# Shift products with the shift columns stationary, and their rows of sums turned by matmuls with ones

## The chip, the core and the metric

The kernel runs on one core of a Trainium2 chip. A core has five engines with queues of their own: TensorE (PE; its weight loads are shown apart as PEld), VectorE (DVE), ScalarE (ACT), GpSimd (POOL) and SyncE (SP), the last mostly for starting DMAs. They wait for one another by semaphores. The metric is the time on the device of one execution, in microseconds; smaller is better.

## What is computed

Two layers of a decoder trunk on 512 tokens of width 1024, in float32. Every layer has three blocks (an FFN, a mixing block with attention and convolution, an FFN), and every block begins with a norm that is scaled and shifted by columns drawn from a vector c:

```python
def rms_norm(x, g):
    xf = x.astype(jnp.float32)
    y = xf * lax.rsqrt(jnp.mean(xf * xf, axis=-1, keepdims=True) + EPS)
    return (y * g.astype(jnp.float32)).astype(x.dtype)

def modulate(h, shift, scale):
    return h * (1 + scale[:, None, :]) + shift[:, None, :]
...
        h = modulate(rms_norm(x, ffn1_norm[l]), sh1, sc1)
        x = x + 0.5 * g1[:, None, :] * swiglu(h, ffn1_w_in[l], ffn1_w_out[l])

        h = modulate(rms_norm(x, mix_norm[l]), sh2, sc2)
        proj = h @ w_mix_in[l]
...
        h = modulate(rms_norm(x, ffn2_norm[l]), sh3, sc3)
        x = x + 0.5 * g3[:, None, :] * swiglu(h, ffn2_w_in[l], ffn2_w_out[l])
```

All matrices are sums of three products of rounded parts, high by high, high by low and low by high, which keeps float32's precision on TensorE's faster float32r path.

## The kernel before

Activations lie turned: 128 channels on the partitions, 512 tokens in the free dimension, `KT` = 8 tiles for the width of 1024. A weight slab is 1024 x 128, held as `[128, 8, 128]`. SP loads it into `raw[slot]`, ScalarE rounds it to `whi[slot]` (`w_hi_part`, L435), VectorE takes the rest into `wlo[slot]` (`w_lo_part`, L790), and TensorE makes 3 x 8 products of 512 columns from it (`slab`, L1501 to L1503). Slabs come in pairs, slot 0 and slot 1; `w_hi`, `w_lo`, `w_used` count them.

Where a block begins (an *entry*), TensorE doesn't wait for the norm. It takes the first pair of slabs on the plain x, scaled by the norm's gain but neither divided by the root nor shifted (`plain_hi`, `plain_lo`). VectorE later multiplies what comes out by the row `RSTD` (`read_bank`, L873), and the shift's part is added as a column for each slab, `wshift` = slab^T times shift. The second pair of an entry takes the real normed and shifted tiles, one "unit" of 128 channels after another: VectorE `unit_gain` (L825), ScalarE `unit_hi` (L454), VectorE `unit_lo` (L834). There are five such entries: mix, second FFN, then in layer 1 first FFN, mix, second FFN.

On TensorE an entry is two calls of `two_slabs` (L1506). Slot 1 runs four steps behind slot 0. In the first call each step holds, besides its three products of 512 columns, two shift products (L1526, L1527): the weight slice (high, then low part) is stationary, and the two columns `SHP[:, shift, n, :]` (high and low part of the shift) move. They sum up in `S[slot][:, 0:2]`; VectorE adds the two columns at the end of its `norm_units` (L910). At k == 3 the mean of the squares is made (`norm_mean`, L1636). Before it can be used there follow ScalarE's root (L442) and VectorE's reciprocal (L814).

VectorE's order in an entry is written out by hand: unit gains and lows 0 to 2, read bank 0, rest of the next weights of slot 0, low of unit 3, read bank 1, gain of unit 4, rest of the weights of slot 1, gain of unit 5, low of unit 4, and so on. ScalarE's order is unit highs with two weight roundings in between (`ENTRY_SPLITS`).

The *first entry* is made otherwise, since the shift comes late (its columns are computed from `ada_w`). Two pairs are done on the plain x (`plain_slabs`), and `third_pair` (L1567) takes the third pair on the units. The shift products of the first two pairs (four slabs, 32 products of two matmuls) are put among its 16 turns, two products to a turn, into the banks `S[0]`, `S[1]`, `O`, `AUX`; in the first four steps two products with a tile of ones (`keep_busy`, L1646) are added at the end of each. After it the loop of FFN tiles begins with `slab(3, 0)`, which writes bank `G[0]` and so waits for `acc_read[0]`. That is counted up by VectorE's L935 in `first_gates`, and before L935 VectorE's queue holds L921 (which waits for ScalarE's tanh, L565), L924, the weights' rest, L928, L930 and L933, in that order.

Of the kernel before, what the change touches and what calls it, by code (L numbers as in the profile page):

```python
# [124 lines left out]
def build(nc, a, onehot, out):  # L125
# [28 lines left out]
    whi = [at(f"w_hi{s}", [P, 8, P], F32R) for s in range(2)]  # L154
    wlo = [at(f"w_lo{s}", [P, 8, P], F32R) for s in range(2)]
# [31 lines left out]
    wshift = at("w_shift", [P, 2], F32)  # L187
    busy = at("busy", [P, TOK], F32R)
# [45 lines left out]
    whi_next = [at(f"w_hi_next{s}", [P, 8, P], F32R, r0 + 64 * KB + s * 4 * KB) for s in range(2)]  # L234
    wlo_next = [at(f"w_lo_next{s}", [P, 8, P], F32R, r0 + 72 * KB + s * 4 * KB) for s in range(2)]
# [183 lines left out]
    def _(act):  # L419
# [36 lines left out]
        def norm_units(l, k, pair):  # L456
# [6 lines left out]
            for j in range(KT):  # L463
# [6 lines left out]
                if j in ENTRY_SPLITS and not first:  # L470
                    w_hi_part(pair + 1, ENTRY_SPLITS[j])

# [84 lines left out]
        for l in range(DEPTH):  # L557
            for w in range(2):
                n_in, n_out = f"ffn{w + 1}_in", f"ffn{w + 1}_out"
                norm_units(l, 2 * w, l * PAIRS + PAIR0[n_in])  # L560
                if l + w == 0:
                    w_hi_part(3, 0, used=1)
                    act.wait_ge(sem("first_gate"), 1)
# [222 lines left out]
    def _(dve):  # L786
# [74 lines left out]
        def norm_units(l, k, pair, rows):  # L861
# [44 lines left out]
            low(7)  # L906
            for t in range(2):
                if first:
                    dve.wait_ge(w_used[t], 1)
                dve.tensor_scalar(wshift[:, t:t + 1], S[t][:, 0:1], S[t][:, 1:2], rows[t], ALU.add, ALU.mult)\  # L910
                    .then_inc(sem("shift_read"), 1)

        def first_gates():
# [15 lines left out]
            dve.wait_ge(w_used[0], 2)  # L929
            dve.tensor_scalar(wshift_next[:, 0:1], O[:, 0:1], O[:, 1:2], 1.0, ALU.add, ALU.mult).then_inc(sem("shift_read_next"), 1)  # L930
# [14 lines left out]
            dve.tensor_scalar(wshift_next[:, 1:2], AUX[:, 0:1], AUX[:, 1:2], 1.0, ALU.add, ALU.mult)\  # L945
                .then_inc(sem("shift_read_next"), 1)
            dve.wait_ge(sem("shift_read_next"), 2)
# [542 lines left out]
    def _(pe):  # L1490
# [14 lines left out]

        def two_slabs(pair, use, ready, shift=None, at={}, banks=G, weights=(whi, wlo)):  # L1506

            lag = 4
            for k in range(KT + lag):
                if k in at:  # L1510
                    at[k]()
                for slot, n in ((1, k - lag), (0, k)):
# [12 lines left out]
                    if shift is not None:  # L1525
                        pe.matmul(S[slot][:, 0:2], wh, SHP[:, shift, n, :], start=n == 0, stop=False)  # L1526
                        pe.matmul(S[slot][:, 0:2], wl, SHP[:, shift, n, :], start=False, stop=n == KT - 1)  # L1527
# [31 lines left out]
        def shift_product(slot, n, out, weights):  # L1559
# [3 lines left out]
            if n == KT - 1:  # L1563
                mm.then_inc(w_used[slot], 1)
# [354 lines left out]
```

## Time and profile before

| | |
|---|---|
| median of 3 runs | 2539.62 us (2538.05 to 2539.93) |
| profiled execution, its own time | 2538.0 us |
| its span | 2536.3 us |
| TensorE busy | 2511.7 us, 99% |
| VectorE busy | 1687.4 us, 67% |
| ScalarE busy | 968.0 us, 38% |
| mean granted TensorE clock | 0.998 |

A matmul's busy time is modelled and overlaps the next one's, so 99% doesn't mean that nothing could be saved; the distance between the starts of two neighbours is what a product costs. A row of the timeline gives start, busy time, engine, line, operation, out<-in, shape and in brackets the idle time before it with what ended it. A row of the chain gives start, length and what the end of the execution hung on then.

### The profile page before, as it was taken

What the parts mean: (1) busy time and instruction counts of PE and PEld (TensorE: products, weight loads), DVE (VectorE), ACT (ScalarE), POOL (GpSimd) and SP (SyncE); (2) the same over time, 40 slices, a digit from 0 to 9 for tenths busy, and PEclk for the clock granted to TensorE, in tenths of its full rate; (3) what the DMA queues carried; (4) which work ended last, traced back from release to release, by engine and by line L of the source; (5) the groups of instructions that cost most, each with busy time, mean ns of one, the idle gap of its engine ahead of it and who ended that gap; (6) DMA issues with size and microseconds to landing.
All of it is one profiled execution on the core that took longest, in us unless ns stands there. A gap on an engine that the chain in (4) does not pass through costs nothing.

```text
span 2536.3 us, 34970 instructions
## 1 busy us (share of the span) xinstructions
PE 2511.7 (99%) x11607; PEld 2049.3 (81%) x11607; DVE 1687.4 (67%) x2531; ACT 968.0 (38%) x1630; POOL 108.2 (4%) x187
## 2 busy tenths in 40 slices
PE   8999999999999999999999999999999999999998
PEld 6888887878788878888878888877877888788887
DVE  8655678899987575643365557788999865634432
ACT  4322324454545342232232332255455443432223
POOL 3000110000000000000000001100000000000000
PEclk9999999999999999999999999999999999999999
DMA  9555574232223435533335556722222333333332
GB/s 279 156 166 158 187 241 119 83 87 82 86 84 91 133 91 159 156 102 97 92 100 158 156 166 191 232 80 83 86 84 79 88 100 94 89 99 96 92 99 86
DMA packets 467654, 310.99 MB, mean 123 GB/s; under 512 B 10891, under 2 KB 445181, under 8 KB 467576
## 3 DMA queue, kind: packets, MB, share of 16 engines
q1 hardware_dynamic: 444544, 234.91, 31.7%
q0 software_dynamic: 20352, 70.13, 8.6%
q10 hardware_dynamic: 2696, 5.13, 0.7%
q8 instruction: 38, 0.62, 0.1%
q14 instruction: 24, 0.20, 0.0%
HBM read 305.41 MB, written 5.05 MB: 122 GB/s over the span
## 4 chain that ended last, share of the span: by engine, by line
PE 92%; DVE 4%; ACT 2%; issue 1%; DMA 1%; POOL 0%; ACTq 0%; DVEq 0%; POOLq 0%
PE bank L1501 28%; PE bank L1503 28%; PE bank L1502 28%; PE bank L1803 2%; PE bank L1781 1%; DVE rstd L814 1%; DVE scaled L825 1%; PE bank L1773 1%; DVE h_lo L834 1%; DVE w_lo L790 1%; PE bank L1523 1%; PE bank L1528 0%; PE bank L1524 0%; PE bank L1811 0%; PE bank L1789 0%
## 5 line engine op out<-in xcount | busy, mean ns | idle before, releaser
L790 DVE TENSOR_TENSOR w_lo<-w_raw,w_hi 128x1024 fp32r<-128x1024 f32 (+1 forms) x428 | 514.9, 1203 | 539.8 <-ACT w_hi L435 539.0
L1501 PE MATMUL bank<-h_hi,w_hi 128*128 128x512 f32 x2096 | 833.3, 398 | 0.3 <-DVE scaled L1150 0.2
L1503 PE MATMUL bank<-h_hi,w_lo 128*128 128x512 f32 x2096 | 817.6, 390 | 0.0
L1502 PE MATMUL bank<-h_lo,w_hi 128*128 128x512 f32 x2096 | 816.3, 389 | 0.0
L435 ACT ACTIVATE w_hi<-w_raw 128x1024 fp32r<-128x1024 f32 (+1 forms) x428 | 445.3, 1040 | 847.3 <-PE bank L1503 796.3
L1501 PEld LDWEIGHTS bank<-h_hi,w_hi 128*128 128x128 f32 x2096 | 393.6, 188 | 85.8 <-issue 4.2
L1503 PEld LDWEIGHTS bank<-h_hi,w_lo 128*128 128x128 f32 x2096 | 393.4, 188 | 84.5
L1502 PEld LDWEIGHTS bank<-h_lo,w_hi 128*128 128x128 f32 x2096 | 394.1, 188 | 77.3 <-issue 0.5
L1266 DVE SCALAR_TENSOR_TENSOR conv_part<-glu,conv_taps,conv_part 128x512 f32<-128x512 f32 x464 | 319.7, 743 | 0.0
L1501 PE MATMUL bank<-s_hi,w_hi 128*128 128x512 f32 x704 | 275.5, 391 | 0.0
L1503 PE MATMUL bank<-s_hi,w_lo 128*128 128x512 f32 x704 | 274.0, 389 | 0.0
L1502 PE MATMUL bank<-s_lo,w_hi 128*128 128x512 f32 x704 | 273.9, 389 | 0.0
L1503 PEld LDWEIGHTS bank<-s_hi,w_lo 128*128 128x128 f32 x704 | 132.2, 188 | 27.7
L1502 PEld LDWEIGHTS bank<-s_lo,w_hi 128*128 128x128 f32 x704 | 132.2, 188 | 26.9
L1501 PEld LDWEIGHTS bank<-s_hi,w_hi 128*128 128x128 f32 x704 | 132.2, 188 | 26.9
L989 DVE SCALAR_TENSOR_TENSOR ada_acc<-ada_raw,c_act,ada_acc 128x1024 f32<-128x1024 f32 x112 | 143.3, 1280 | 0.9
L389 POOL DMA_DIRECT2D ada_raw<-in_ada_w x128 | 69.0, 539 | 1153.0 <-DVE ada_acc L986 544.5
L594 ACT ACTIVATE s_hi<-full 128x512 f32 (+1 forms) x82 | 51.9, 632 | 162.4 <-DVE full L1158 162.4
L1160 DVE TENSOR_TENSOR s_lo<-full,s_hi 128x512 f32 (+1 forms) x82 | 56.8, 692 | 73.9 <-ACT s_hi L594 73.9
L494 ACT ACTIVATE squares<-x_res 128x512 f32 (+1 forms) x48 | 30.3, 632 | 194.6 <-DVE x_res L972 194.6
L677 ACT ACTIVATE probs<-probs,neg_row_max 128x512 f32<-128x512 f32 (+3 forms) x128 | 71.0, 556 | 74.2 <-DVE neg_row_max L1303 73.9
L972 DVE SCALAR_TENSOR_TENSOR x_res<-bank,gates,x_res 128x512 f32 (+1 forms) x48 | 36.0, 751 | 68.0 <-PE bank L1503 67.8
(271 smaller groups left out, 2682.7 us busy)
## 6 DMA issues: line engine op xcount, KB each, us to landing
w_raw<-in_ffn_w_in SPq DMA_DIRECT2D x176, 512.0 KB, 3.9
ada_raw<-in_ada_w POOLq DMA_DIRECT2D x128, 512.0 KB, 4.8
w_raw<-in_w_mix_in SPq DMA_DIRECT2D x112, 512.0 KB, 3.7
w_raw<-in_ffn_w_out SPq DMA_DIRECT2D x64, 512.0 KB, 3.9
w_raw<-in_ffn_w_out SPq DMA_DIRECT2D x32, 384.0 KB, 3.5
ada_first<-in_ada_w SPq DMA_DIRECT2D x16, 512.0 KB, 9.0
w_raw<-in_w_attn_branch SPq DMA_DIRECT2D x16, 512.0 KB, 3.8
w_raw<-in_w_conv_branch SPq DMA_DIRECT2D x16, 512.0 KB, 3.8
```

The lines of the kernel that those rows point to most:

```text
L389: pool.dma_start(ada_raw[k % 4][:, :], w_ada[:, ds(layer * KT + k, 1), ds(m * D, D)].rearrange("p o f -> p (o f)"))\
L435: act.activation(whi[slot][:, 0:n, :], raw[slot][:, 0:n, :], ACT.Copy).then_inc(w_hi[slot], 1)
L594: act.activation(tile(SHI2, i), F[0][:, :], ACT.Copy).then_inc(sem("s_hi"), 1)
L677: act.activation(PR[par][m][:, 0:n], PR[par][m][:, 0:n], ACT.Exp, bias=nmx[:, par, m:m + 1], scale=-1.0, accum_out=rsum[:, par, m:m + 1]). ...
L790: dve.tensor_tensor(wlo[slot][:, 0:n, :], raw[slot][:, 0:n, :], whi[slot][:, 0:n, :].bitcast(F32), ALU.subtract).then_inc(w_lo[slot], 1)
L989: ins = dve.scalar_tensor_tensor(out=ACC[:, :], in0=ada_raw[k % 4][:, :], scalar=CA[:, k:k + 1], in1=ACC[:, :], op0=ALU.mult, op1=ALU.add)
L1160: dve.tensor_tensor(tile(SLO2, i), F[0][:, :], tile(SHI2, i).bitcast(F32), ALU.subtract)\
L1266: ins = dve.scalar_tensor_tensor(out=CAB[t % 2][:, :], in0=Z[:, t:t + TOK], scalar=wt, in1=CAB[t % 2][:, :], op0=ALU.mult, op1=ALU.add)
L1501: pe.matmul(acc, wh, hi[:, k0 + k, :], start=first and k == 0, stop=False)
L1502: pe.matmul(acc, wh, lo[:, k0 + k, :], start=False, stop=False)
L1503: mm = pe.matmul(acc, wl, hi[:, k0 + k, :], start=False, stop=last and k == n - 1)
L1803: mm = pe.matmul(S[m][:, 0:n], q[m * HD:(m + 1) * HD, i * P:(i + 1) * P], k[m * HD:(m + 1) * HD, 0:n], start=term == 0, stop=term == 2)
```

## The change

The roles of the two operands are exchanged. The two shift columns of a tile are stationary now, and 256 weight columns, 128 of each slot, move. The result is two rows of 256 sums, for the high and the low part of the shift, in `S[0][0:2, 0:256]`. ScalarE copies them to SBUF, and two matmuls with two of the ones of `busy` turn each slot's 2 x 128 block into a column of 128 and add its two rows. For this the weight tiles of the two slots lie in one tensor, `w_both`.

In the entries the eight tiles' products (two matmuls each) stand at k = 5, 6 and 7 of the first call of `two_slabs`; ScalarE's copy stands after unit 4; the two turning matmuls (`entry_sums`) stand at k == 6 of the second call, into `S[1][:, 0:2]`, where VectorE reads them after the last unit. In the first entry turns 0 to 3 of `third_pair` take two tiles each of the first pair's weights and turns 4 to 11 one tile each of the second's, with one `keep_busy` instead of two. There the first copy is at unit 4 and `entry_sums` at k == 6. The second copy stands in ScalarE's queue between the rounding of pair 3, slot 0, and the tanh, and waits for turn 11; its two matmuls stand at k == 10.

```diff
@@ sbuf
-    whi = [at(f"w_hi{s}", [P, 8, P], F32R) for s in range(2)]
-    wlo = [at(f"w_lo{s}", [P, 8, P], F32R) for s in range(2)]
+    w_both = [at(f"w_{part}", [P, 2, 8, P], F32R) for part in ("hi", "lo")]
+    whi, wlo = [[both[:, s, :, :] for s in range(2)] for both in w_both]
@@ scalar, norm_units
                 if j in ENTRY_SPLITS and not first:
                     w_hi_part(pair + 1, ENTRY_SPLITS[j])
+                if j == KT // 2:
+                    if first:
+                        act.wait_ge(w_used[1], 1)
+                    else:
+                        act.wait_ge(sem("shift_rows"), l * 3 + k)
+                    act.activation(shift_rows[0:2, :], S[0][0:2, 0:2 * P], ACT.Copy).then_inc(sem("shift_rows_copied"), 1)
@@ scalar, first FFN
                 if l + w == 0:
                     w_hi_part(3, 0, used=1)
+                    act.wait_ge(w_used[1], 2)
+                    act.activation(shift_rows_next[0:2, :], O[0:2, 0:2 * P], ACT.Copy).then_inc(sem("next_rows_copied"), 1)
                     act.wait_ge(sem("first_gate"), 1)
@@ vector, norm_units
+            dve.wait_ge(sem("shift_sums"), l * 3 + k + 1)
             for t in range(2):
-                if first:
-                    dve.wait_ge(w_used[t], 1)
-                dve.tensor_scalar(wshift[:, t:t + 1], S[t][:, 0:1], S[t][:, 1:2], rows[t], ALU.add, ALU.mult)\
-                    .then_inc(sem("shift_read"), 1)
+                dve.tensor_scalar(wshift[:, t:t + 1], S[1][:, t:t + 1], rows[t], None, ALU.mult).then_inc(sem("shift_read"), 1)
@@ vector, first_gates
-            dve.wait_ge(w_used[0], 2)
-            dve.tensor_scalar(wshift_next[:, 0:1], O[:, 0:1], O[:, 1:2], 1.0, ALU.add, ALU.mult).then_inc(sem("shift_read_next"), 1)
+            dve.wait_ge(sem("next_sums"), 1)
+            dve.tensor_copy(wshift_next[:, :], AUX[:, 0:2]).then_inc(sem("shift_read_next"), 1)
...
-            dve.tensor_scalar(wshift_next[:, 1:2], AUX[:, 0:1], AUX[:, 1:2], 1.0, ALU.add, ALU.mult)\
-                .then_inc(sem("shift_read_next"), 1)
-            dve.wait_ge(sem("shift_read_next"), 2)
@@ tensor
+        def shift_product(n, shift, out, weights):
+
+            pe.matmul(out[0:2, 0:2 * P], SHP[:, shift, n, :], weights[0][:, :, n, :], start=n == 0, stop=False)
+            return pe.matmul(out[0:2, 0:2 * P], SHP[:, shift, n, :], weights[1][:, :, n, :], start=False, stop=n == KT - 1)
+
+        def shift_sums(out, rows):
+
+            for t in range(2):
+                mm = pe.matmul(out[:, t:t + 1], rows[0:2, t * P:(t + 1) * P], busy[0:2, 0:1].bitcast(F32), start=True, stop=True)
+            return mm
+
+        def entry_sums(n):
+
+            pe.wait_ge(sem("shift_rows_copied"), n + 1)
+            shift_sums(S[1], shift_rows).then_inc(sem("shift_sums"), 1)
@@ tensor, two_slabs
+                if shift is not None and lag < k < KT:
+                    for n in range(3 * (k - lag - 1), min(3 * (k - lag), KT)):
+                        mm = shift_product(n, shift, S[0], w_both)
+                    if k == KT - 1:
+                        mm.then_inc(sem("shift_rows"), 1)
...
-                    if shift is not None:
-                        pe.matmul(S[slot][:, 0:2], wh, SHP[:, shift, n, :], start=n == 0, stop=False)
-                        pe.matmul(S[slot][:, 0:2], wl, SHP[:, shift, n, :], start=False, stop=n == KT - 1)
@@ tensor, third_pair
+                if k == 6:
+                    entry_sums(0)
+                if k == 10:
+                    pe.wait_ge(sem("next_rows_copied"), 1)
+                    shift_sums(AUX, shift_rows_next).then_inc(sem("next_sums"), 1)
...
-                    for part in range(2):
-                        i = 2 * turn + part
-                        out, pair_weights = products[i // KT]
-                        shift_product(i // KT % 2, i % KT, out, pair_weights)
-                        if part == 0:
-                            pe.matmul(acc, wh, HLO[:, n, :], start=False, stop=False)
+                    if turn < lag:
+                        for m in (2 * turn, 2 * turn + 1):
+                            last = shift_product(m, 0, S[0], w_both)
+                        if turn == lag - 1:
+                            last.then_inc(w_used[0], 1)
+                    elif turn < lag + KT:
+                        last = shift_product(turn - lag, 0, O, next_both)
+                        if turn == lag + KT - 1:
+                            last.then_inc(w_used[0], 1)
+                    rest = pe.matmul(acc, wh, HLO[:, n, :], start=False, stop=False)
+                    if turn in (lag - 1, lag + KT - 1):
+                        rest.then_inc(w_used[1], 1)
...
                     if k < lag:
-                        keep_busy(2, S[1])
+                        keep_busy(1, S[1])
@@ tensor, entry
-                      banks=G if name == "mix" else TP)
+                      at={6: lambda: entry_sums(n)}, banks=G if name == "mix" else TP)
```

## Rows read from the trace of the kernel before

**Rows 1.** The page's part 4: shares of the chain by engine.

```profile
PE 92%; DVE 4%; ACT 2%; issue 1%; DMA 1%; POOL 0%; ACTq 0%; DVEq 0%; POOLq 0%
```

**Rows 2.** Chain in order of time (start, length, what), l0 mix entry.

```profile
403.69 0.76 DVE x_res L972
...
423.18 0.67 DVE h_lo L834
...
423.90 0.50 PE bank L1523
...
431.85 0.29 issue
```

**Rows 3.** The same chain in the l1 ffn2 entry.

```profile
2155.21 0.76 DVE x_res L972
...
2175.30 0.50 PE bank L1523
```

**Rows 4.** Timeline (start, busy, what) of TensorE, first pair of an entry.

```profile
404.25 0.40 PE L1523 MATMUL bank<-h_hi,w_hi 128*128 128x512 f32 x1
...
405.17 0.39 PE L1523 MATMUL bank<-h_hi,w_hi 128*128 128x512 f32 x1
...
418.61 0.48 PE L1528 MATMUL bank<-h_hi,w_lo 128*128 128x512 f32 x1
419.56 0.47 PE L1523 MATMUL bank<-h_hi,w_hi 128*128 128x512 f32 x1 [0.48 <-issue]
```

**Rows 5.** Timelines of TensorE, VectorE and ScalarE, first entry.

```profile
54.20 0.47 PE L1581 MATMUL bank<-h_hi,w_hi_third 128*128 128x512 f32 x1 [0.95 <-DVE h_lo L834]
...
65.25 0.39 PE L1581 MATMUL bank<-h_hi,w_hi_third 128*128 128x512 f32 x1
...
66.39 0.39 PE L1581 MATMUL bank<-h_hi,w_hi_third 128*128 128x512 f32 x1
...
74.32 0.39 PE L1501 MATMUL bank<-h_hi,w_hi 128*128 128x512 f32 x1
...
60.84 0.75 DVE L834 SCALAR_TENSOR_TENSOR h_lo<-scaled,modulation,h_hi 128x512 fp32r<-128x512 f32 x1
...
68.58 0.68 DVE L921 SCALAR_TENSOR_TENSOR scaled<-scaled,full 128x512 f32<-128x512 f32 x1
...
72.36 0.68 DVE L935 SCALAR_TENSOR_TENSOR scaled<-scaled,bank 128x512 f32<-128x512 f32 x1
...
66.25 0.63 ACT L565 ACTIVATE scaled<-full 128x512 f32<-128x512 f32 x1
```

**Rows 6.** Timeline of TensorE around score products of 256 and 128 columns.

```profile
478.59 0.28 PE L1803 MATMUL bank<-k_lo,q_hi 64*128 64x256 f32 x2
478.70 0.28 PE L1803 MATMUL bank<-k_hi,q_lo 64*128 64x256 f32 x2
...
484.78 0.39 PE L1503 MATMUL bank<-h_hi,w_lo 128*128 128x512 f32 x1
...
485.92 0.39 PE L1502 MATMUL bank<-h_lo,w_hi 128*128 128x512 f32 x1
```

**Rows 7.** ScalarE: a group by line and shape (busy, mean ns), and its timeline.

```profile
L643 ACT ACTIVATE weights_t<-bank 128x256 f32<-128x256 f32 x16 | 6.2, 385 | 6.5 <-PE bank L1773 6.5
...
423.27 0.72 ACT L454 ACTIVATE h_hi<-scaled,modulation 128x512 fp32r<-128x512 f32 x1 [1.07 <-DVE scaled L825]
```

**Rows 8.** One line's instructions: ns min/median/max, first and last start, L1889.

```profile
L1889 PE MATMUL bank<-inv_d,squares x8: 250/250/271, 2526.6 to 2527.4; 128*128 128x1 f32 x8
```

**Rows 9.** Timelines of VectorE and TensorE, end of the l0 mix entry.

```profile
431.35 0.68 DVE L1342 TENSOR_TENSOR k_lo<-squares,k_hi 128x512 fp32r<-128x512 f32 x1
...
432.13 0.50 PE L1803 MATMUL bank<-k_hi,q_hi 64*128 64x512 f32 x2 [0.29 <-issue]
```

**Rows 10.** Stretches: busy us of each engine, granted clock, DMA share, GB/s.

```profile
13.00:15.50 2.50, 0.07 (x1) 0.00 (x0) 2.25 (x2) 0.00 (x0) 0.00 (x0) 1.00 1.04 386
16.00:20.00 4.00, 4.00 (x16) 3.14 (x14) 3.83 (x4) 0.51 (x1) 0.00 (x0) 0.57 1.03 410
```

More of the change, by code:

```diff
@@ L187, in build @@
     wshift = at("w_shift", [P, 2], F32)
+    shift_rows = at("shift_rows", [P, 2 * P], F32)
     busy = at("busy", [P, TOK], F32R)
@@ L232, in build @@
     CAB = [at(f"conv_part{i}", [P, TOK], F32, z0 + 2176 + 2 * KB * i) for i in range(2)]
-    whi_next = [at(f"w_hi_next{s}", [P, 8, P], F32R, r0 + 64 * KB + s * 4 * KB) for s in range(2)]
-    wlo_next = [at(f"w_lo_next{s}", [P, 8, P], F32R, r0 + 72 * KB + s * 4 * KB) for s in range(2)]
+    next_both = [at(f"w_{part}_next", [P, 2, 8, P], F32R, r0 + (64 + i * 8) * KB) for i, part in enumerate(("hi", "lo"))]
+    whi_next, wlo_next = [[both[:, s, :, :] for s in range(2)] for both in next_both]
+    shift_rows_next = at("shift_rows_next", [P, 2 * P], F32, r0 + 62 * KB)
     whi_third = [at(f"w_hi_third{s}", [P, 8, P], F32R, r0 + 16 * KB + s * 4 * KB) for s in range(2)]
@@ L1557, in plain_slabs, with third_pair @@
                         mm.then_inc(sem("plain_read"), 1)
-        def shift_product(slot, n, out, weights):
-            pe.matmul(out[:, 0:2], weights[0][slot][:, n, :], SHP[:, 0, n, :], start=n == 0, stop=False)
-            mm = pe.matmul(out[:, 0:2], weights[1][slot][:, n, :], SHP[:, 0, n, :], start=False, stop=n == KT - 1)
-            if n == KT - 1:
-                mm.then_inc(w_used[slot], 1)
-        def third_pair(banks, weights, products):
+        def third_pair(banks, weights):
             lag = 4
@@ L1581, in third_pair @@
                     pe.matmul(acc, wh, HHI[:, n, :], start=n == 0, stop=False)
-                    for part in range(2):
-                        i = 2 * turn + part
-                        out, pair_weights = products[i // KT]
-                        shift_product(i // KT % 2, i % KT, out, pair_weights)
-                        if part == 0:
-                            pe.matmul(acc, wh, HLO[:, n, :], start=False, stop=False)
+                    if turn < lag:
[10 more added lines that the diff above has]
+                        rest.then_inc(w_used[1], 1)
                     mm = pe.matmul(acc, wl, HHI[:, n, :], start=False, stop=n == KT - 1)
-                    turn += 1
                     if n == KT - 1:
@@ L1592, in third_pair @@
                     if k < lag:
-                        keep_busy(2, S[1])
+                        keep_busy(1, S[1])
+                    turn += 1
         def first_entry():
@@ L1604, in first_entry @@
             pe.wait_ge(sem("aux_read"), 1)
-            third_pair(G, thirds, ((S[0], (whi, wlo)), (S[1], (whi, wlo)), (O, nexts), (AUX, nexts)))
+            third_pair(G, thirds)
         def entry(l, k, name):
```

## The prediction

> **What bounds the kernel now.** I read the page's chain first [rows 1]: TensorE carries 92% of it, so taking matmuls away looks like taking time away. That share is an average. I therefore took the chain in order of time in the two kinds of place that the edit touches: the five entries (l0 mix at 403 us, l0 ffn2 at 912, l1 ffn1 at 1279, l1 mix at 1647, l1 ffn2 at 2155) and the first entry at 54 to 74 us.
>
> In an entry [rows 2] the chain leaves TensorE when the last x tile is updated at 403.69, goes through root, reciprocal and the unit scalings on ScalarE and VectorE, and comes back to TensorE only at 423.90, when the fifth unit's low part (begun 423.18) is there. From 423.90 on, the second pair of slabs is the chain to its end at 431.85. The other four entries have the same links; the last goes from 2155.21 to 2175.30 [rows 3], 20.1 us as against 20.2. The shift products that go lie in the *first* pair, inside the stretch in which VectorE sets the end. TensorE finishes that pair about 0.5 us early: its last product starts at 418.61, and the next pair's first at 419.56 after 0.48 us idle [rows 4]. In the first entry it is the reverse: TensorE is the chain without a gap from 54.20 to 74.32 [rows 5].
>
> **Change, part by part. The entries, first pair.** A step (slot, k) with its two shift products takes 405.17 - 404.25 = 0.92 us [rows 4]; a plain product is 0.23 (from the chain [rows 2]: 431.85 less 423.90, less 0.50 for the first, over 32), so the two 2-column products cost 0.23 together, 0.115 each, and 32 of them 3.7 us. In their place stand 16 products of 256 columns. The nearest rows are the score products with 256 moving columns: neighbours start at 478.59 and 478.70, 0.11 apart [rows 6]. They have a 64-row stationary block and run as two side by side, so that it is the step of a pair; I take 0.115, 1.8 us in all. TensorE is done some 1.9 us sooner, but the second pair's fifth step still waits for 423.9. **Worth nothing**: next late after TensorE is VectorE's fixed order, which waits nowhere for TensorE in this stretch. ScalarE's copy of the two rows (2 x 256; the nearest row, 128 x 256 out of a bank, takes 0.385 [rows 7]) goes between unit 4 and unit 5, where ScalarE sat idle 1.07 us for VectorE [rows 7]: hidden; without that cover it would cost 0.4 on the chain.
>
> **The entries, second pair.** New at k == 6, in the middle of the chain: two matmuls that turn the rows. They are plain f32; such a one runs as two instructions (the means at the end: 8 for 4 matmuls, last start 0.8 after first, 0.115 each [rows 8]), so four of them are 0.46. Their stationary block has 2 of 128 rows. The nearest rows for a block of few rows amid full ones are the last scores: from the product at 484.78 to the next but one at 485.92 is 1.14 us, where two plain steps are 0.46 and the three side-by-side pairs of 128 columns 0.34; 0.34 is left for going over and back [rows 6]. So the sums cost 0.46 to 0.80; being narrow I take 0.80. A waiting bubble of some 0.08 at unit 6 and another after the pair, where TensorE waited for VectorE, swallow up to 0.15.
> The Trainium skill, "TensorEngine Tiling (Array Packing)", Key Properties, says that a change of the array's tiling mode drains the engine; that speaks against this change, and the 0.34 above agrees. Against it, "TensorE: Matmul & The Clock Gate", Back-to-back issue gap, gives a floor of about 25 ns for small matmuls by themselves, by which the four would be an estimated 0.1 us; the row of the means shows 115 ns with a load for each, so the sum goes by the row. By the page's floor the entries would add nothing and the whole would come to about 2539, inside the range.
> - Three ffn entries: about +0.6 each, **+1.8**. VectorE's readers of the sums come after the last unit, over 0.5 us behind TensorE's k == 6, so the wait for them holds up nothing.
> - Two mix entries: after the pair the score products already waited for k_lo (431.35 + 0.68 = 432.03) and began at 432.13 [rows 9], 0.28 after the chain says that the pair was through [rows 2]. Of 0.65 some 0.25 is left, twice: **+0.4**. Bound for all five: 0 to +4.0.
>
> **The first entry.** Before, a step is 66.39 - 65.25 = 1.14 us [rows 5]: three products and four of 0.115. After, turns 0 to 3 have four of the new ones and one busy product instead of two: 0.69 + 0.46 + 0.23 = 1.38. With turn 4 that is 54.20 + 4 x 1.38 + 0.92 = 60.6, so turn 5 still starts when unit 4 is low (60.84 + 0.75, so about 61.7 [rows 5]). Seven turns at 0.92 and the sums, 0.8, bring turn 11 to about 68.9; four bare steps and the second sums end the pair near 72.4 instead of 74.32. Taken alone, 1.9 us gained. But the change puts a wait in ScalarE's queue: after w_hi of pair 3, slot 0, it waits for w_used[1] of turn 11 and then copies the rows (68.9 + 0.385, so 69.25). **Queued behind it** is the first tanh (66.25 before), and behind that VectorE's L921 (68.58) and, by a fixed row of instructions, L935 (72.36 to 73.04), which alone frees bank G[0] for TensorE's next slab [rows 5]. Tanh at 69.25 and 0.63 long puts L921 at 69.95, 1.35 late, and L935's end at 74.4. TensorE starts the next slab at 74.5 instead of 74.32: **+0.2**, not -1.9. The gain is traded for a wait. Bounds: with sums at 0.46 it is -0.15; with dearer products, below.
>
> Sum: 1.8 + 0.4 + 0.2 = +2.4 us, on the profiled execution's 2538.0 (span 2536.3 and 1.7 around it) 2540.4. That execution was 1.6 under the median of the three runs, 2539.6; against the median **2542.0 us**. About 5 us, 0.2%, is what a measurement of this kernel can tell from no change.
>
> **Rivals.**
> 1. *TensorE is the bound everywhere.* Then every freed slot counts: per entry -3.7 + 1.8 + 0.8 = -1.1, five times -5.4; in the first entry 64 x 0.115 and 4 busy products less 32 x 0.115 and twice 0.8, so -3.0. Total -8.4: 2531. For it the 92% [rows 1]; against it the entries' chain and its slack, which show who is waited for [rows 2 to 5]. Chance 0.06.
> 2. *The clock.* (The slower side.) From 13.08 to 15.50 TensorE stood still, and the granted clock, full until then, was 0.57 in the mean from 16 to 20 us although TensorE was busy throughout [rows 10]: the lower level, 1.2 GHz, for most of it, and 0.43 x 4 = 1.7 us of work lost. Later, up to its last work, TensorE's longest pause is the 0.95 us at 54.20 [rows 5]. The change makes longer ones: 1.9 us before the second pair in each entry, 2.0 us before slab 3 in the first. If the clock falls, an entry loses up to 1.7 less the slack of its first steps (423.90 - 419.56 for 15 products at 0.23, so 0.9), so about 1.0, and the first entry 1.7: 2542.0 + 5 + 1.7 = 2548.7; in the first alone, 2543.7. It decides only if the clock answers these pauses as it did that one, which was longer (2.4 us) and stood among sparser work. Chance of the full form 0.15.
> 3. *The 2-column stationary block costs a change of mode too.* 0.34 per group: hidden in the entries (three groups, 1.0 us, of 1.9), but in the first entry twelve groups: turns 0 to 3 at 1.72 end near 61.1, eight turns at 1.26 and the sums near 71.9, 3.0 later than above: 2545.0. The same comes out if a new product takes 0.2. The 2-column moving form can't show it. Chance 0.11.
> 4. *The sums run at the low end and the bubbles take most:* 2540. Part of the forecast's range.
>
> **How the numbers follow.** Forecast, with rival 4 in it: 0.66; rival 1: 0.06; rival 2: 0.15; rival 3: 0.11; 0.02 for none of these. Range: from the forecast without its terms, 2538.5, to just short of the full clock case, 2548.0; rival 1 and half of rival 2 are left out. Slower by over 5 us (above 2544.7): most of rival 2, half of rival 3, 0.17; faster by as much (under 2534.5): rival 1, 0.05; within: 0.78.
>
> **What would show it.** The chain of after must again leave TensorE from the x update to unit 4's low part, 20.2 us in each entry; TensorE must show a pause near 1.9 us before the second pair. The 256-column products must start 0.11 to 0.12 apart, the four sum instructions must widen k == 6 by 0.5 to 0.8. In the first entry the tanh of L565 must start near 69.2 behind the copy, and TensorE stand idle from about 72.4 until the bank is free near 74.4. A granted clock under 1.00 after 60 us would mean rival 2; an L935 end near 77, rival 3. A second pair beginning its fifth step sooner than 20.2 us after the x update would overturn the reading of the entries.

## The result and the profile after

| | before | after |
|---|---|---|
| median | 2539.09 us (2537.74 to 2540.60, 17 runs) | 2543.48 us (2541.71 to 2545.91, 17 runs) |
| profiled execution, its own time | 2538.0 us | 2541.71 us |
| its span | 2536.3 us | 2539.7 us |
| mean granted clock | 0.998 | 0.998 |

The changed kernel takes 1.0016 of the time before (95% interval 1.0008 to 1.0023), so +4.4 us between the medians, against +2.4 forecast over a base of 2539.6. It is slower, by a little less than the 5 us that the prediction had called measurable; the interval leaves out 1, so that threshold was set too high.

The page of the changed kernel, its busy times and the shares of its chain by engine:

```profile
PE 2504.5 (99%) x11519; PEld 2032.6 (80%) x11519; DVE 1686.7 (66%) x2530; ACT 969.7 (38%) x1637; POOL 108.4 (4%) x187
...
PE 91%; DVE 5%; ACT 2%; issue 1%; DMA 1%; POOL 0%; ACTq 0%; DVEq 0%; POOLq 0%
```

TensorE's busy time went down by 7.2 us and the span went up by 3.4. Where, is seen as for before [rows 1 to 5]. The chain of the changed kernel in the l0 mix entry (start, length, what):

```profile
404.34 0.76 DVE x_res L977
...
423.82 0.67 DVE h_lo L844
424.54 0.49 PE bank L1549
...
426.95 0.53 PE bank L1519 x4
```

From the x update to the second pair's fifth step are again 20.20 us (424.54 - 404.34), as before [rows 2]: nothing of TensorE's saving came through. The last row is new. It is the sums, on the chain.

TensorE's timeline of the same entry (start, busy time, what, idle time before and its releaser):

```profile
406.75 1.10 PE L1663 MATMUL bank<-running_sum,inv_d 128*128 128x512 f32 x2 [0.56 <-issue]
...
409.78 0.28 PE L1513 MATMUL bank<-w_hi,shift_parts 128*2 128x256 f32 x1
409.89 0.28 PE L1514 MATMUL bank<-w_lo,shift_parts 128*2 128x256 f32 x1
...
418.30 0.39 PE L1551 MATMUL bank<-h_hi,w_lo 128*128 128x512 f32 x1
420.21 0.47 PE L1549 MATMUL bank<-h_hi,w_hi 128*128 128x512 f32 x1 [1.52 <-DVE w_lo L800]
...
426.56 0.40 PE L1551 MATMUL bank<-h_hi,w_lo 128*128 128x512 f32 x1
426.88 0.60 PE L1519 MATMUL bank<-busy,shift_rows 2*128 2x1 f32 x4
...
427.75 0.40 PE L1550 MATMUL bank<-h_lo,w_hi 128*128 128x512 f32 x1
...
433.07 0.50 PE L1830 MATMUL bank<-k_hi,q_hi 64*128 64x512 f32 x2
```

Six of the new products fill 409.78 to 410.47 (the next plain product), 0.115 each. The freed time stands as idle time in two places: 0.56 at 406.75, where the mean now has to be waited for and before stood no wait (counted from start to start, 405.80 to 406.75, it is 0.95 where a plain step is 0.23, so 0.72), and 1.52 ahead of the second pair instead of 0.48 [rows 4]. From the product before the sums to the second one behind them are 1.19 us (427.75 - 426.56) where two plain steps are 0.46: the sums cost 0.73.

The first entry in the changed kernel, rows of TensorE, VectorE and ScalarE, as in [rows 5]:

```profile
54.86 0.47 PE L1602 MATMUL bank<-h_hi,w_hi_third 128*128 128x512 f32 x1 [1.41 <-DVE h_lo L844]
...
72.90 0.39 PE L1615 MATMUL bank<-h_hi,w_lo_third 128*128 128x512 f32 x1
75.26 0.47 PE L1506 MATMUL bank<-h_hi,w_hi 128*128 128x512 f32 x1 [1.97 <-DVE scaled L943]
...
70.61 0.69 DVE L929 SCALAR_TENSOR_TENSOR scaled<-scaled,full 128x512 f32<-128x512 f32 x1 [1.06 <-ACT scaled L575]
...
74.33 0.68 DVE L943 SCALAR_TENSOR_TENSOR scaled<-scaled,bank 128x512 f32<-128x512 f32 x1
...
69.60 0.37 ACT L572 ACTIVATE shift_rows_next<-bank 2x256 f32<-2x256 f32 x1 [2.51 <-PE bank L1612]
69.88 0.62 ACT L575 ACTIVATE scaled<-full 128x512 f32<-128x512 f32 x1
```

TensorE starts 0.66 later than in [rows 5] (54.86, not 54.20). Its start follows ScalarE's rounding of an earlier tile of weights, which waits for that tile to land, by 19.9 us in every profile. Before, then changed:

```profile
34.28 1.06 ACT L423 ACTIVATE w_hi_next<-w_raw 128x1024 fp32r<-128x1024 f32 x1 [0.62 <-DMA w_raw<-in_ffn_w_in]
34.94 1.06 ACT L425 ACTIVATE w_hi_next<-w_raw 128x1024 fp32r<-128x1024 f32 x1 [1.09 <-DMA w_raw<-in_ffn_w_in]
```

The edit doesn't touch that transfer. Yet of the five profiles of the kernel before and of its variants below, four start the entry at 54.13 to 54.73 and one at 56.09, and the nine of the change and its variants at 54.60 to 55.27. Whether the change moves the landing stays open. Counted from the entry's start, the next slab begins after 20.40 us instead of 20.12.

With that the profile's +3.4 us closes: 0.66 for the start, 0.28 for the first entry, -0.29 from there to the l0 mix x update (329.08 instead of 329.37), and 2.75 from that update to the end (2135.36 instead of 2132.61).

### The profile page after: what moved, and what is told of

It reads as the page before. It is cut to its first block, busy times and chain, and to the rows that moved or that the text cites. A ratio compares the mean times of both kernels' runs of the same rounds, so it can differ in the third digit from the quotient of the medians.

```text
span 2539.7 us, 34799 instructions
## 1 busy us (share of the span) xinstructions
PE 2504.5 (99%) x11519; PEld 2032.6 (80%) x11519; DVE 1686.7 (66%) x2530; ACT 969.7 (38%) x1637; POOL 108.4 (4%) x187
## 4 chain that ended last, share of the span: by engine, by line
PE 91%; DVE 5%; ACT 2%; issue 1%; DMA 1%; POOL 0%; ACTq 0%; DVEq 0%; POOLq 0%
PE bank L1506 28%; PE bank L1508 28%; PE bank L1507 28%; PE bank L1830 2%; PE bank L1808 1%; DVE rstd L824 1%; DVE scaled L835 1%; DVE h_lo L844 1%; DVE w_lo L800 1%; PE bank L1800 1%; PE bank L1549 1%; PE bank L1551 0%; PE bank L1550 0%; PE bank L1838 0%; PE bank L1816 0%
## 5 line engine op out<-in xcount | busy, mean ns | idle before, releaser
L800 DVE TENSOR_TENSOR w_lo<-w_raw,w_hi 128x1024 fp32r<-128x1024 f32 (+1 forms) x428 | 514.9, 1203 | 542.4 <-ACT w_hi L437 541.6
L994 DVE SCALAR_TENSOR_TENSOR ada_acc<-ada_raw,c_act,ada_acc 128x1024 f32<-128x1024 f32 x112 | 143.3, 1280 | 0.9
```

Source lines behind the costliest of these rows:

```text
L800: dve.tensor_tensor(wlo[slot][:, 0:n, :], raw[slot][:, 0:n, :], whi[slot][:, 0:n, :].bitcast(F32), ALU.subtract).then_inc(w_lo[slot], 1)
L994: ins = dve.scalar_tensor_tensor(out=ACC[:, :], in0=ada_raw[k % 4][:, :], scalar=CA[:, k:k + 1], in1=ACC[:, :], op0=ALU.mult, op1=ALU.add)
```

## The experiments

Three sets were timed against the kernel before, each set on one chip, and one pair for profiles alone. Of the 101 executions of the kernel before, five lay at 2557 us; a profile of one stands under what was unexpected, and the medians are untouched by them.

**Is TensorE the bound in the entries after all (rival 1)?** In the kernel before, only tile 0's shift products are left in the five entries, so the shift is not the full one:

```diff
-                    if shift is not None:
+                    if shift is not None and n == 0:
```

> The kernel before, in whose five entries only tile 0 of the eight keeps its shift products (4 of 32 matmuls with 2 moving columns for each entry stay); the other tiles' part of the shift column is left out of the result. The theory (the entry's first pair lies under VectorE's chain): no time gained beyond 0.3 us, from the x update to the second pair's fifth step again 20.1 to 20.2 us in every entry, only TensorE's pause before the second pair grows from 0.5 to some 3.7 us. The rival (TensorE is the bound everywhere): 28 x 0.115 x 5 = 16 us faster than before. The clock's rival: the pause of 3.7 us brings the granted clock down behind it in some entries, at most 1.0 to 1.7 us each, so up to 8 us slower than before.

Measured: 2543.06 us (2541.85 to 2562.95, 11 runs), ratio 1.0015 (1.0005 to 1.0024). With 28 of an entry's 32 small matmuls gone, the kernel is *slower*. The pause ahead of the second pair grows to 3.3 us, and behind it the granted clock is half. TensorE's timeline in the l0 mix entry, and a stretch behind the pause (busy us of each engine, granted clock, DMA share, GB/s); this execution ran 18 us late, for the reason given at the end:

```profile
435.23 0.39 PE L1528 MATMUL bank<-h_hi,w_lo 128*128 128x512 f32 x1
438.87 0.77 PE L1523 MATMUL bank<-h_hi,w_hi 128*128 128x512 f32 x1 [3.26 <-DVE w_lo L790]
...
439.00:442.00 3.00, 3.00 (x8) 2.32 (x8) 3.00 (x5) 0.72 (x1) 0.00 (x0) 0.50 0.52 143
```

The same fall stood in all five entries, twice as long in l1 mix as in the others. The fifth step comes 20.96 us after the x update (443.96 - 423.00), not 20.2 as expected, since the first products behind the pause stand 0.43 apart and not 0.23. That leaves two readings: the freed slots are worth nothing and the clock costs the time by which the kernel is slower (3.8 us), or they are worth something and the clock takes more. So the pause was filled, with 24 products of ones that nothing reads:

```diff
+                      at={0: lambda: busy_part(12, TP[1])},
```

> The kernel before with the shift products of tile 0 alone in the five entries (fourteen pairs of them left out of each entry, so the shift is not the full one), and in the pause that opens ahead of each second pair 24 products of ones with 256 columns, 2.8 of the 3.3 us, read by nothing. The same without the filling gave 2543.06, 3.8 over the kernel before, with half-speed stretches of 3.41 us after the pauses of all five entries. Theory (the entries are bounded by VectorE's row, and the 3.8 us were the clock's): with the pauses filled there is no half-speed stretch after 60 us, and the time is that of the kernel before within 1 us, so 2538.5 to 2540.5. Rival (TensorE's freed slots are worth time, and the clock's fall merely hid it): clearly under the kernel before, down to 16 us.

Measured: 2538.72 us (2538.04 to 2539.82, 10 runs), ratio 0.9997 (0.9988 to 1.0007), and the granted clock is full from 17 us to the last work. TensorE in the l0 mix entry:

```profile
419.73 0.28 PE L1652 MATMUL bank<-busy 128*128 128x256 f32 x1
420.41 0.47 PE L1523 MATMUL bank<-h_hi,w_hi 128*128 128x512 f32 x1 [0.41 <-issue]
...
424.75 0.50 PE L1523 MATMUL bank<-h_hi,w_hi 128*128 128x512 f32 x1 [0.34 <-DVE h_lo L834]
```

The fifth step comes 20.21 us after the x update (424.75 - 404.54), products or no products, and the whole entry takes what it took before (table below). So the entries hang on VectorE, and rival 1 is out.

The 3.8 us were not the clock's alone. By the table the five entries of the unfilled run are 2.6 us longer than before. The same profile has two waits for late weights behind them, 1.20 us at 1037.72 and 1.41 at 1406.46, of the kind that is taken up under "What varies"; the filled run has none over 0.2 there. How much of the medians' difference is either's isn't separated.

**Are the entries' sums the loss?** They are moved into TensorE's pause, from k == 6 to k == 0 of the second pair, and ScalarE's copy from unit 4 to unit 1:

```diff
-                if j == KT // 2:
+                if j == (KT // 2 if first else 1):
...
-                      at={6: lambda: entry_sums(n)}, banks=G if name == "mix" else TP)
+                      at={0: lambda: entry_sums(n)}, banks=G if name == "mix" else TP)
```

> The changed kernel with the turning matmuls of the five entries moved from k == 6 of the second pair, in TensorE's chain, to its start, in TensorE's pause; ScalarE's copy goes from behind unit 4 to behind unit 1. The theory (the sums' place costs 0.66 us in an ffn entry and 0.3 in a mix entry): 3 x 0.66 + 2 x 0.3 = 2.6 us less than the changed kernel, some 1.5 us over before. The rival (the products and the first entry cost it): no difference from the changed kernel, 4 us over before.

Measured: 2539.92 us (2539.18 to 2542.45, 11 runs), ratio 1.0004 (0.9995 to 1.0013). The timeline shows them where TensorE waits for VectorE anyway:

```profile
420.23 0.39 PE L1551 MATMUL bank<-h_hi,w_lo 128*128 128x512 f32 x1
420.55 0.60 PE L1519 MATMUL bank<-busy,shift_rows 2*128 2x1 f32 x4
422.15 0.47 PE L1549 MATMUL bank<-h_hi,w_hi 128*128 128x512 f32 x1 [1.01 <-DVE w_lo L800]
```

The whole loss in the entries is the place of four small instructions: by the table below the five entries take no longer than before. The gain, 3.6 us against the changed kernel's 2543.5, is 0.7 more than the 2.8 by which the table has the entries shorter than in the change. The runs of one kernel spread over 3 to 5 us, so a difference of 0.7 between sets isn't read.

The counter-proof, the entries' sums made twice:

```diff
+            if n:
+                shift_sums(S[1], shift_rows)
```

> The changed kernel with the turning matmuls of the five entries done twice in a row at k == 6. If the price is in the matmuls (0.115 each with its load), the four extra instructions add 0.46 in each entry, 2.3 us over the changed kernel, all of it on the chain; if it is all in each one's narrow block, 0.80 each, 4.0 us; if the sums are nearly free (25 ns each), 0.5 us.

Measured: 2546.10 us (2543.98 to 2547.02, 10 runs), 2.6 over the 2543.5 of the change; by the table 2.2 in the entries, against 2.3 expected. In its l0 mix entry:

```profile
428.89 0.39 PE L1553 MATMUL bank<-h_hi,w_lo 128*128 128x512 f32 x1
429.21 1.05 PE L1519 MATMUL bank<-busy,shift_rows 2*128 2x1 f32 x8
...
430.52 0.40 PE L1552 MATMUL bank<-h_lo,w_hi 128*128 128x512 f32 x1
```

1.63 us (430.52 - 428.89) instead of 1.19: four more cost 0.44, so 0.11 each, and of the 0.73 some 0.27 is paid once for a group.

**Is that 0.27 the narrow block?** The entries' two rows are put in a tile of 128 rows whose other 126 POOL sets to zero once, so that the block is 128 by 128:

```diff
+            m = P if rows is shift_rows else 2
...
-                mm = pe.matmul(out[:, t:t + 1], rows[0:2, t * P:(t + 1) * P], busy[0:2, 0:1].bitcast(F32), start=True, stop=True)
+                mm = pe.matmul(out[:, t:t + 1], rows[0:m, t * P:(t + 1) * P], busy[0:m, 0:1].bitcast(F32), start=True, stop=True)
```

> The change, with the two rows of sums in a tile of 128 rows whose other 126 are zero, so that the four sum instructions of each entry have a stationary block of 128 by 128 in place of 2 by 128. In the change, the step with the sums is 1.19 us long where two plain products are 0.46: 0.73, of it 0.46 for four instructions at 0.115 and 0.27 for something else. Theory A (the 0.27 is the way into a block of 2 rows and back): the step shrinks to about 0.92, five times 0.27 less where nothing hides it, so 0.8 to 1.3 us under the change. Theory B (it comes with any small f32 product amid the large ones): the same step and the same time.

Measured: 2541.18 us (2540.58 to 2543.83, 12 runs), beside 2543.79 (2540.57 to 2545.23, 12 runs) for the change itself in the same set:

> The change as it is, run beside the next three so that they are compared on one chip. Theory (what the trace of it showed: 0.65 for the sums in each of three ffn entries, 0.3 in each of two mix entries, 0.4 in the first entry, 0.3 outside the span, and a part that varies from run to run): 2543.5, within 0.7.

```profile
427.00 0.39 PE L1554 MATMUL bank<-h_hi,w_lo 128*128 128x512 f32 x1
427.23 0.50 PE L1522 MATMUL bank<-busy,shift_rows 128*128 128x1 f32 x4
...
427.92 0.40 PE L1553 MATMUL bank<-h_lo,w_hi 128*128 128x512 f32 x1
```

0.92 us (427.92 - 427.00), 0.27 less: going over to a block of 2 rows and back is what it cost (both operands have 128 rows now, so the run doesn't tell the stationary one from the moving one), and four small f32 instructions by themselves are 0.46. The Trainium skill, "TensorEngine Tiling (Array Packing)", Key Properties, has the array drain at a change of mode, which agrees with these 0.27 if a block of 2 rows counts as another mode; the trace doesn't name modes.

The medians differ by 2.6 us, twice what was expected (0.8 to 1.3); drawing runs anew from both, by 0.4 to 3.5. They bear out the direction only. The size is read from the entries. From the x update to TensorE's first product behind the second pair (scores in the mix entries, the next slab in the others), us, in one profile each:

| | l0 mix | l0 ffn2 | l1 ffn1 | l1 mix | l1 ffn2 | sum over before |
|---|---|---|---|---|---|---|
| before | 28.44 | 27.89 | 27.92 | 28.46 | 27.90 | |
| changed | 28.73 | 28.55 | 28.58 | 28.77 | 28.56 | +2.58 |
| sums early | 28.32 | 27.89 | 27.93 | 28.32 | 27.90 | -0.25 |
| sums twice | 29.21 | 28.99 | 28.99 | 29.21 | 29.00 | +4.79 |
| full rows | 28.49 | 28.29 | 28.29 | 28.49 | 28.29 | +1.24 |
| tile 0 alone | 28.53 | 28.35 | 28.36 | 29.61 | 28.35 | +2.59 |
| tile 0 alone, pause filled | 28.45 | 27.89 | 27.92 | 28.45 | 27.91 | +0.01 |

The two further profiles of the kernel before and the two of the change repeat their rows within 0.04 us.

**Does ScalarE's copy hold up the first entry?** It is put behind the tanh and the next weights' rounding:

```diff
                     w_hi_part(3, 0, used=1)
-                    act.wait_ge(w_used[1], 2)
-                    act.activation(shift_rows_next[0:2, :], O[0:2, 0:2 * P], ACT.Copy).then_inc(sem("next_rows_copied"), 1)
...
                     w_hi_part(3, 1, used=1)
+                    act.wait_ge(w_used[1], 2)
+                    act.activation(shift_rows_next[0:2, :], O[0:2, 0:2 * P], ACT.Copy).then_inc(sem("next_rows_copied"), 1)
```

> The changed kernel with ScalarE's second copy of rows (and its wait for turn 11) moved behind the first tanh and the rounding of pair 3, slot 1. The theory: VectorE's first product with the tanh no longer waits for it and starts about 1.1 us sooner, so does the reading of bank 0, and TensorE's next slab starts near 74.2 instead of 75.3: 1.1 us less than the changed kernel, its pause 0.9 instead of 2.0 us. The rival (the bank was held by the row of VectorE's instructions, not by the copy): no difference.

Measured: 2541.89 us (2540.81 to 2545.78, 11 runs), 1.6 under the change. Rows of ScalarE, VectorE and TensorE (this execution begins the entry at 55.27):

```profile
67.03 1.06 ACT L437 ACTIVATE w_hi<-w_raw 128x1024 fp32r<-128x1024 f32 x1 [1.31 <-DMA w_raw<-in_ffn_w_in]
68.00 0.61 ACT L573 ACTIVATE scaled<-full 128x512 f32<-128x512 f32 x1
...
68.13 1.23 DVE L800 TENSOR_TENSOR w_lo<-w_raw,w_hi 128x1024 fp32r<-128x1024 f32 x1 [0.96 <-ACT w_hi L437]
...
70.47 0.68 DVE L929 SCALAR_TENSOR_TENSOR scaled<-scaled,full 128x512 f32<-128x512 f32 x1
...
75.11 0.47 PE L1506 MATMUL bank<-h_hi,w_hi 128*128 128x512 f32 x1 [1.41 <-DVE scaled L943]
```

The tanh starts 12.7 us after the entry's start instead of 15.0, but VectorE is then late itself: L929 follows L926 with no gap, 15.2 instead of 15.75, and the slab comes after 19.84 us instead of 20.40. So 0.56 came of the move, half of the 1.1 expected. VectorE's row was late because its L800 waited 0.96 for a tile of weights that landed later here: that rounding starts 11.8 us after the entry's start, in the change 11.2. In the change's own profile VectorE stood idle for 1.06 ahead of L929, which is what the move could give with the weights landing as there. The other 1.0 between the medians has a candidate in the next point: the pause is 1.41 us here, not 1.97.

**The clock in the first entry.** In the changed kernel TensorE stands still for 1.97 us ahead of the slab. Seven products of ones go in there:

```diff
             third_pair(G, thirds)
+            keep_busy(7, S[0])
```

> The change, with seven more products of ones at the end of the first entry's pair (their result is read by nothing), so that TensorE works through 1.6 of the 2.0 us for which it waits for the bank of the next slab. Theory A (the clock falls after this pause in a good part of the executions, as it did in the profiles of the runs with the sums early and with the sums twice, and not in those of the change itself and of the copy later): no half-speed stretch after 60 us, and a median 0.5 to 1.5 us under that of the change. Theory B (the clock plays no part in the median; what varies is something else): the same as the change within 0.4 us, or 0.1 more.

Measured: 2542.65 us (2541.54 to 2543.57, 12 runs). That is 1.1 under the change in the same set; drawing runs anew from both, the difference of the medians lies between -2.0 and +0.6, so the medians alone don't settle whether the clock plays a part in them, and the one profile of this run, at full clock, doesn't either, since the change's first two are so too. A third profile of the changed kernel was taken, with one of the kernel before:

> A third profile of the changed kernel, for the same question. Theory A: the loop of l0 ffn2 takes anywhere from 367.2 to 369.0. Theory B: 367.9 to 369.0, with the wait for late weights.

> A third profile of the kernel before. In the loop of l0 ffn2 (from the x update near 913 us to the one near 1280 us) the two profiles of it took 366.5 and 366.9 us and showed no wait for late weights over 0.2 us; the changed kernel and its variants, their own 0.65 us for the sums taken off, took 366.7 to 368.3 and showed a wait of 1.0 to 1.5 us in seven of eight. Theory A (chance of the execution): this profile falls anywhere in 366.5 to 368.3. Theory B (it goes with the changed kernel): 366.5 to 367.0 again.

The former took 2545.3 us. Two stretches of it behind the pause (its slab starts at 75.52 after 1.97 us):

```profile
77.00:79.00 2.00, 2.00 (x6) 1.54 (x5) 1.96 (x8) 1.04 (x2) 0.00 (x0) 0.50 0.01 2
81.00:84.00 3.00, 3.00 (x15) 2.47 (x14) 0.00 (x1) 1.10 (x2) 1.54 (x3) 1.00 0.76 239
```

At 1.2 GHz for a few microseconds: from the slab to the l0 mix x update it needs 330.75 us (406.27 - 75.52), where the first profile needs 329.08 (404.34 - 75.26) and the second 329.21, at full clock throughout. So 1.6 us, and the two profiles of variants in which it fell there need 330.97 and 330.96. With a pause of 1.97 to 2.42 us it fell in three of six profiles (this one, the sums early, the sums twice) and not in the other three (the two of the change, the full rows); with 1.41 us (copy later), 0.39 (filled) or none it did not, in one profile each.

**What varies in the loop of l0 ffn2.** From its x update near 913 us to the next near 1280, the profiles of the kernel before take 366.5, 366.9 and 366.8 us, those of the changed one 367.4, 368.3 and 368.9. The sums explain 0.65. The rest is one wait of TensorE, at 1016 to 1023, for weights that landed late. The second profile of the kernel before answers first:

> The kernel before as it is, for a second profile of it. In the profiles of every kernel of the two sets before this one TensorE waits once for 1.0 to 1.5 us near 1015 us in the loop of l0 ffn2, where a tile of weights lands late; neither of the first two profiles has that. Theory A (it comes with the chip or the execution, whatever the kernel): this profile has it too. Theory B (the change brings it): it has not.

It and the third of before have no such wait over 0.2 us, so theory B seemed to hold, for the kernel before and for the change's second and third profile (1.1 and 1.6 us), though not for its first (none over 0.2). The transfers tell more. In every profile POOL starts four transfers of `ada_raw` (2 MB) here, and SP two of weights just behind, and they share the engines. The change, second profile: the queue of instruction transfers from 1010 to 1012 (packets, MB, share), ScalarE at the landing, and TensorE behind it:

```profile
q8 instruction: 1, 0.02, 3.2%
...
1016.32 1.06 ACT L437 ACTIVATE w_hi<-w_raw 128x1024 fp32r<-128x1024 f32 x1 [5.26 <-DMA w_raw<-in_ffn_w_in]
...
1019.48 0.47 PE L1506 MATMUL bank<-h_hi,w_hi 128*128 128x512 f32 x1 [1.08 <-DVE scaled L1155]
```

The kernel before, second profile, ScalarE at the same two places:

```profile
1006.48 1.06 ACT L435 ACTIVATE w_hi<-w_raw 128x1024 fp32r<-128x1024 f32 x1 [3.96 <-PE bank L1503]
1014.35 1.06 ACT L435 ACTIVATE w_hi<-w_raw 128x1024 fp32r<-128x1024 f32 x1 [4.19 <-DMA w_raw<-in_ffn_w_in]
```

From one rounding to the next are 7.87 us here and 8.94 in the change (the first of its two at 1007.38). A packet of 0.02 MB of instructions falls into the crowd in all nine profiles of the change and its variants, and in none of before's three; both kernels have six such packets from 912 to 1290, at other places. But the run with tile 0's shift products alone, which has nothing of the change, has a packet there too, and a wait of 1.2 us; the same with its pause filled has neither. So it goes with where the code of a kernel is refilled, not with what the change does: 1.0 to 1.6 us in nine of the ten profiles with the packet, at most 0.2 in the four without. This is a match between profiles; no run moved that packet alone.

Nor is the wait the change's own. The l0 first FFN has the same crowd of transfers from 132 us on, and there it is the kernel before that has a packet, at 135.3, and the change that has none. TensorE in the second profile of the kernel before:

```profile
141.17 0.47 PE L1501 MATMUL bank<-h_hi,w_hi 128*128 128x512 f32 x1 [1.18 <-DVE scaled L1150]
```

Its other two profiles wait 0.20 and under 0.15 us there, the two runs with tile 0's products 1.30 and 0.38, the nine of the change and its variants at most 0.31. So a packet in the crowd goes with a long wait often and not always, and each kernel has its own places for it.

**A version that keeps the new products and loses the waits.** Both moves above, and on VectorE the readers of the two plain banks behind the one that frees the next slab's bank:

```diff
-            dve.tensor_tensor(OT[:, :], TP[0][:, :], RSTD[:, :], ALU.mult).then_inc(sem("second_read"), 1)
-            dve.tensor_tensor(BT[:, :], TP[1][:, :], RSTD[:, :], ALU.mult).then_inc(sem("second_read"), 1)
...
             dve.tensor_tensor(SLO[:, 0, :], F[0][:, :], SHI[:, 0, :].bitcast(F32), ALU.subtract).then_inc(sem("s_lo"), 1)
+            dve.wait_ge(sem("g_tanh"), 2)
+            dve.scalar_tensor_tensor(out=T[1][:, :], in0=T[0][:, :], scalar=1.0, in1=G[0][:, :],
+                                     op0=ALU.add, op1=ALU.mult).then_inc(acc_read[0], 1)
+            dve.tensor_tensor(OT[:, :], TP[0][:, :], RSTD[:, :], ALU.mult).then_inc(sem("second_read"), 1)
+            dve.tensor_tensor(BT[:, :], TP[1][:, :], RSTD[:, :], ALU.mult).then_inc(sem("second_read"), 1)
```

> The change with three moves: the entries' sums in TensorE's pause ahead of the second pair; ScalarE's copy of the second rows behind the first tanh; and on VectorE the two readers of the plain banks (o_t, bias_tile) behind the one that frees the bank of the next slab, which then waits for the tanh of the second slot alone. Theory: sums early 3.6 under the change (measured), copy later 1.6 under it (measured); the bank is freed near 73 us in place of 75, the pair of the first entry ends near 73.3, so that TensorE gains up to 1.5 more unless a later reader of the plain banks falls behind. 2537.5 to 2538.5, about 1 to 2 under the kernel before. Rival (the moves take gains from one another, since the clock's share is in each): 2539 to 2540, no better than the sums early alone.

Measured: 2537.70 us (2536.84 to 2538.34, 12 runs), ratio 0.9987 (0.9975 to 0.9999): 6.1 under the change and 1.9 under the kernel before. VectorE and TensorE in the first entry (begun at 54.60):

```profile
71.03 0.68 DVE L936 SCALAR_TENSOR_TENSOR scaled<-scaled,bank 128x512 f32<-128x512 f32 x1
71.63 0.68 DVE L938 TENSOR_TENSOR o_t<-bank,rstd 128x512 f32<-128x512 f32 x1
...
72.63 0.39 PE L1615 MATMUL bank<-h_hi,w_lo_third 128*128 128x512 f32 x1
72.85 0.39 PE L1506 MATMUL bank<-h_hi,w_hi 128*128 128x512 f32 x1
```

The slab follows the pair without a pause, 18.25 us after the start instead of 20.12. That is the 1.9 us that the new products save where TensorE is the chain. That the medians differ by the same 1.9 is in part chance: the profiled execution, the slowest of the twelve, also has a wait of 1.44 us for late weights and 0.3 more around its span.

## Why the prediction came out as it did

No difference of 5 us, and a little slower: that was the forecast, and the time lies in its range, 1.5 us above the 2542.0 that it named. By its steps:

- *The entries, first pair, worth nothing*: right. 20.20 us from x update to fifth step, and the run with the pauses filled shows that even 28 of 32 small matmuls less change nothing. The products' price was right (0.115). TensorE ended the pair only about 1.0 us sooner, not 1.9: 0.72 went into the wait for the mean, a wait that the prediction didn't see. It cost nothing, since TensorE has to stand still ahead of the second pair anyway.
- *The entries, second pair*: right. The sums cost 0.73, inside 0.46 to 0.80; the 0.34 from the score products was 0.27 here. An ffn entry grew by 0.66 (from x update to the loop's first slab 28.55 us, 941.58 - 913.03, against 27.89), forecast 0.6; the mix entry by 0.29, forecast 0.2. All five: 3 x 0.66 + 2 x 0.29 = 2.6, forecast 2.2.
- *The first entry*: right link by link. From the entry's start: copy 14.74 (forecast 14.7), tanh 15.02 (15.05), L921's successor 15.75 (15.75), the slab 20.40 (20.3). +0.28 against +0.2. The copy's wait wasn't the only obstacle to the 1.9 us, though: VectorE's own row stood 0.6 to 1.1 us behind it, and only with its two readers moved as well did the slab come 1.87 sooner than before.
- *Rival 1* (0.06): refuted. *Rival 3* (0.11): did not occur; the 2-column block costs no change of mode, twelve groups stand at 0.115 a product.
- *Rival 2, the clock* (0.15 for its full form): the full form did not occur; 1.52 us of pause in the entries never brought the clock down. Its small form, in the first entry alone, came in part of the executions, 1.6 us each time. The prediction named it at 2543.7, but had no half case. With three in six, an estimate from six profiles, it adds some 0.8 us to a typical run. The mean clock on record of each run gives no more than a hint. In the set with the full rows the change took 2544.4 us (median of eight) where that clock is 0.998 and 2541.8 (of four) where it is 0.999; in the runs of the result it took 2543.6 and 2543.4.

The edit's own terms were sized well: +2.4 forecast, +2.8 measured (2.56 + 0.28). What the sum put too low lies outside them. The clock was left at nothing in it and is worth an estimated 0.8. Late weights were no term at all: the change has 1.1 us of them in a typical profile, the kernel before 0.2, so some 0.9. The time around the span was taken over as 1.7 us and is 2.0 in all runs of the change and its variants; why isn't shown. Together 4.8 where 4.4 was measured, and some 0.4 more if the later start of the first entry is the change's. The clock's and the weights' shares come from a few profiles, so the sum is no closer than that. The base mattered too: the three runs shown had their median 0.5 above that of the 17, which hid 0.5 of the miss. That the time lies near the forecast is thus partly luck: 2.8 of the 4.4 us came by the mechanism forecast.

## What to carry to other kernels

When an edit frees an engine that is busy 99% of the time, look in the chain at each place it touches for the engine that is waited for; fewer matmuls freed 7.2 us of busy time here and the end came no sooner. A small added piece belongs in the pause that the edit itself opens: the sums cost 2.6 us of the profile in the middle of the critical pair and nothing some 6 us earlier. In a queue written out by hand, after taking away one wait look at what is then late next, and put first whatever frees the resource that the bounding engine needs; of the versions run, only the one with all three moves gave a saving.

## What was unexpected of the hardware

**Clock.** It answers pauses of about 2 us in some executions and not in others of the same kernel, at the same place and pause (1.97 us: full clock twice, half once); after 3.1 to 3.3 us it fell in all five entries of the one profile with such pauses.

**A long stretch at half speed.** Five of 101 executions of the kernel before lay at 2557 us. One was profiled (2557.76 us); two stretches of it, from the first entry on:

```profile
60.00:90.00 30.00, 30.00 (x98) 25.74 (x97) 15.28 (x24) 7.01 (x10) 0.00 (x0) 0.50 0.36 102
97.00:120.00 23.00, 23.00 (x103) 19.06 (x102) 11.42 (x13) 6.49 (x8) 3.86 (x7) 1.00 0.73 232
```

TensorE, busy throughout, is granted 1.2 GHz for more than 30 us, and the l0 mix x update comes at 422.98, 18.5 later than in the profile before it (404.51). The pause ahead was 1.59 us, no longer than in profiles without it. It stood at the same place in the profiled execution of the run with tile 0's products alone. What starts it stays open.

**A narrow block.** A group with a stationary block of 2 rows cost 0.27 us more than the same group with 128 rows, which is more than half of its four instructions (0.46). A block of 2 *columns* cost nothing extra: those products stand 0.115 apart, and so does the plain product behind them.
